# Splitting the last row block of three stage boundaries into halves of the tokens

## What is computed

```python
def rmsnorm(x, g):
    xf = x.astype(jnp.float32)
    y = xf * lax.rsqrt(jnp.mean(xf * xf, axis=-1, keepdims=True) + EPS)
    return y.astype(x.dtype) * g

def swiglu(x, w_gate, w_up, w_down):
    return (jax.nn.silu(x @ w_gate) * (x @ w_up)) @ w_down

# first block
h = h + 0.5 * rmsnorm(swiglu(rmsnorm(h, ffn1_pre_g), w1_gate, w1_up, w1_down), ffn1_post_g)   # then boundary 1
u = rmsnorm(h, mix_pre_g);  ... = split(u @ w_in)            # state-space branch, attention branch, gates
h = h + rmsnorm(merged @ w_out, mix_post_g)                                                   # then boundary 2
h = h + 0.5 * rmsnorm(swiglu(rmsnorm(h, ffn2_pre_g), ...), ffn2_post_g)                       # then boundary 3
# second block
u = rmsnorm_2(h, norm1_g);  proj = u @ w_in_2                # delta rule, sparse attention, gates, FFN
...
return rmsnorm_2(h, final_g)
```

## Time and profile before

| | us |
|---|---|
| time, median of 3 runs | 2542.17 (2541.75 to 2544.55) |
| profiled execution | 2541.03 |
| its span in the trace | 2539.2 |
| TensorE busy in the span | 2491.9 |
| VectorE, ScalarE busy | 1672.5, 1200.7 |
| mean granted TensorE clock | 0.997 of full |

### The profile page before, as it was taken

One profiled execution on the slowest core, in us unless ns is written; L12 is line 12 of the kernel. 1 busy time (PEld: TensorE's weight loads), 2 busy tenths in 40 slices (PEclk: granted clock), 3 DMA queues, 4 the chain that ended last, 5 costly groups with the idle time before them and its releaser, 6 DMA issues.

```text
span 2539.2 us, 37185 instructions
## 1 busy us (share of the span) xinstructions
PE 2491.9 (98%) x15074; PEld 2049.0 (81%) x15074; DVE 1672.5 (66%) x2651; ACT 1200.7 (47%) x1997; POOL 76.1 (3%) x114
## 2 busy tenths in 40 slices
PE   9999999999999999999999999999999999999998
PEld 7999878887877777877999878777776787888887
DVE  6888248856766656248887257766877666677733
ACT  6556235665536455346555246544333454444421
POOL 0111000000000000000110000000000000000000
PEclk9999999999999999999999999999999999999999
DMA  5776322222222212223775323211111221222232
GB/s 172 175 185 152 106 93 92 83 75 75 75 67 75 75 59 72 94 92 92 180 177 154 95 90 100 76 43 35 43 43 51 67 67 63 96 100 96 92 100 71
DMA packets 80523, 237.79 MB, mean 94 GB/s; under 512 B 8928, under 2 KB 10976, under 8 KB 80352
## 3 DMA queue, kind: packets, MB, share of 16 engines
q1 hardware_dynamic: 68832, 213.56, 26.1%
q0 software_dynamic: 10080, 18.35, 4.8%
q10 hardware_dynamic: 1440, 3.49, 0.4%
HBM read 233.27 MB, written 2.10 MB: 93 GB/s over the span
## 4 chain that ended last, share of the span: by engine, by line
PE 85%; DVE 9%; ACT 3%; issue 1%; DMA 1%; ACTq 0%; DVEq 0%; SPq 0%
PE bank L2084 20%; PE bank L2086 19%; PE bank L2085 19%; PE bank L2098 4%; PE bank L2100 4%; PE bank L2099 4%; PE bank L2328 2%; PE bank L2167 1%; DVE hl L2829 1%; DVE small L3184 1%; PE bank L2253 1%; ACT hl L2473 1%; ACT fB L2450 1%; DVE fB L3180 1%; PE bank L2234 1%
## 5 line engine op out<-in xcount | busy, mean ns | idle before, releaser
L2829 DVE TENSOR_TENSOR hl<-raw,hl 128x1024 fp32r<-128x1024 f32 (+2 forms) x325 | 386.0, 1191 | 471.5 <-ACT hl L2473 470.3
L2084 PE MATMUL bank<-uR,hl 128*128 128x512 f32 x1696 | 691.5, 408 | 2.8 <-DVE uR L2840 2.3
L2086 PE MATMUL bank<-uR,hl 128*128 128x512 f32 x1696 | 662.7, 391 | 0.0
L2085 PE MATMUL bank<-uR,hl 128*128 128x512 f32 x1696 | 662.1, 390 | 0.0
L2473 ACT CAST hl<-raw 128x1024 fp32r<-128x1024 f32 (+2 forms) x325 | 329.9, 1020 | 218.4 <-PE bank L2086 212.0
L2084 PEld LDWEIGHTS bank<-uR,hl 128*128 128x128 f32 x1696 | 319.1, 188 | 95.6 <-issue 25.2
L2086 PEld LDWEIGHTS bank<-uR,hl 128*128 128x128 f32 x1696 | 318.8, 188 | 68.8
L2085 PEld LDWEIGHTS bank<-uR,hl 128*128 128x128 f32 x1696 | 319.2, 188 | 68.0 <-issue 7.2
L2823 DVE TENSOR_TENSOR hl<-raw,hl 128x1024 fp32r<-128x1024 f32 (+1 forms) x142 | 150.7, 1075 | 31.5 <-ACT hl L2469 27.8
L2098 PE MATMUL bank<-sum,hl 128*128 128x256 f32 x560 | 159.0, 284 | 1.2 <-DVE fA L2975 1.1
L2099 PE MATMUL bank<-sum,hl 128*128 128x256 f32 x560 | 158.4, 283 | 0.0
(11 more groups left out here) (502 smaller groups left out, 4240.1 us busy)
## 6 DMA issues: line engine op xcount, KB each, us to landing
raw<-in_win SPq DMA_DIRECT2D x147, 512.0 KB, 3.5
raw<-in_w SPq DMA_DIRECT2D x44, 512.0 KB, 3.4
raw<-in_w1u SPq DMA_DIRECT2D x54, 256.0 KB, 3.1
raw<-in_w2u SPq DMA_DIRECT2D x51, 256.0 KB, 3.4
raw<-in_w1g SPq DMA_DIRECT2D x22, 512.0 KB, 4.6
raw<-in_w2g SPq DMA_DIRECT2D x22, 512.0 KB, 4.6
raw<-in_w1d SPq DMA_DIRECT2D x16, 512.0 KB, 3.6
raw<-in_wssd SPq DMA_DIRECT2D x16, 512.0 KB, 3.4
```

The lines of the kernel that those rows point to most:

```text
L2084: e.matmul(s.bank[:, :], h[:, 0, w], hi, start=s.first and q == 0, stop=False)
L2085: e.matmul(s.bank[:, :], h[:, 0, w], lo, start=False, stop=False)
L2086: i = e.matmul(s.bank[:, :], h[:, 1, w], hi, start=False, stop=s.last and q == n - 1)
L2829: e.tensor_tensor(h[:, 1, w], x[:, w], h[:, 0, w].bitcast(F), ALU.subtract).then_inc(*sig("dve_split.lo", s, i))
```

## The change

At the three boundaries the last row block is computed for tokens 0 to 255 (call it half 0) and then for tokens 256 to 511 (half 1), with matmuls of 256 columns. The norm, the residual, the new input `uR` and the three leading panels go by these halves too. `keep(3)` is gone, `sum_first` and `post_fold` are replaced, and `collect` takes pairs of pages that lie in one tensor, so that a VectorE instruction can take two blocks of one half at once. New in the plan, in this order:

```diff
+    def mm_half(p, half, js, xs, bank, cut=slice(None)): ...   # ends[js[p]] = s, 0
+    def post_steps(T, half, pairs, at=()):
+        for n in range(5):
+            if n < 4:
+                ks = (2 * n, 2 * n + 1)
+                T["h"][half][n] = s = step("post_h", ks=ks, ..., last=T["last"][half], qs=T["qs"] if half else None, cols=halves[half])
...
+            if n:
+                T["lo"][half][n - 1] = s = step("post_lo", ks=(2 * n - 2, 2 * n - 1), ..., hi=T["h"][half][n - 1])
...
+            if n in at:
+                open_split(*at[n])
+    def half_sum(T, half):
+        s = step("last_sq", b=T["b"][half], bt=list(T["b"][half].t), q=T["q"], cols=halves[half])
+    def half_root(T, half, ready):
+        s = step("end_sum", b=T["sum"][half], q=T["q"], ready=ready, r=T["r"], cols=halves[half])
+    def last_rows(ys, tail, gpost, half, gpre):
...
+        for p in range(len(js)):
+            if p == len(js) - 1:
+                mm_half(p, 0, js, xs, T["b"][0], slice(0, 4))
+                for n in range(2):
+                    s = step("end_first", b=T["sum"][n], c=acc, cols=halves[n])
+                acc.release(("pe_end.first", s))
+                a_end = mm_half(p, 0, js, xs, T["b"][0], slice(4, None))
+            else:
+                mm_half(p, 0, js, xs, T["b"][0])
+        T["q"], T["r"] = fp.take(), fp.take()
+        sq = half_sum(T, 0)
+        mm_half(0, 1, js, xs, T["b"][1], slice(0, 4))
+        T["rt"][0], _ = half_root(T, 0, sq)
+        b_end = mm_half(0, 1, js, xs, T["b"][1], slice(4, None))
+        for p in range(1, len(js)):
+            b_end = mm_half(p, 1, js, xs, T["b"][1])
...
+        post_steps(T, 0, 4, {0: (js[0] + NHL,), 1: (js[0] + NHL + 1,)} if len(js) > 1 else {})
+    def boundary(T, srcs, normed, drop=None, con=None):
+        sq = half_sum(T, 1)
+        T["rt"][1], done = half_root(T, 1, sq)
+        js = [panel(srcs[0], KB * 128, False)]
+        open_split(js[0] + 2)
...
+        post_steps(T, 1, 4)
```

The engines' parts. On TensorE `lead` keeps its first lines, the wait for the splits of all three panels, and then:

```diff
+            def block(i, half, k):
...
+                e.matmul(b[:, cols], h[:, 0, w], uR[:, 0, k, cols], start=k == 0, stop=False)
+                e.matmul(b[:, cols], h[:, 1, w], uR[:, 0, k, cols], start=False, stop=False)
+                go.wait_ge(*on("dve_norm.lo", lo, k))
+                return e.matmul(b[:, cols], h[:, 0, w], uR[:, 1, k, cols], start=False, stop=k == KB - 1)
+            for i, ks in ((0, range(0, 6)), (2, range(0, 6)), (0, range(6, 8)), (2, range(6, 8))):
+                for k in ks:
+                    for n in ((0, 1), (), (2,))[i]:
+                        block(n, 0, k)
             for k in range(KB):
+                for n in range(3):
+                    i = block(n, 1, k)
+                    if k == KB - 1:
+                        i.then_inc(*sig("pe_gemm.mm", s, n))
```

ScalarE's `post_h` waits for the residual and writes two high parts of 256 columns; in half 1 it also squares both blocks, 512 wide. VectorE's `post_h` and `post_lo`:

```diff
+        def post_h(s):
...
+            if k < KB - 2:
+                i = e.tensor_tensor(y2, y2, two_r, ALU.mult)                  # two blocks x 256 tokens
+            else:
+                e.tensor_tensor(s.ys[k][:, s.cols], s.ys[k][:, s.cols], s.r[:, s.cols], ALU.mult)
+                i = e.scalar_tensor_tensor(out=s.ys[k + 1][:, s.cols], in0=s.b[:, s.cols], ...)
+            e.scalar_tensor_tensor(out=hT[:, k:k + 2, s.cols], in0=y2, scalar=0.5 if s.half else 1.0,
+                                   in1=hT[:, k:k + 2, s.cols], op0=ALU.mult, op1=ALU.add)
+        def post_lo(s):
+            for k in s.ks:
+                go.wait_ge(*on("act_norm.hi", s.hi, k))
+                e.scalar_tensor_tensor(out=uR[:, 1, k, s.cols], in0=hT[:, k, s.cols], ...)
```

More of the change, by code:

```diff
@@ L479, in build, with wide_pages, take_two, both_of @@
     open_split(0, 2)
+    def wide_pages(x, n):
+        bs = [x[:, i, :] for i in range(n)]
+        home.update({id(b): (x, i) for i, b in enumerate(bs)})
+        return bs
+    def take_two():
+        spots = [home[id(b)] for b, _ in fp.left]
+        for n, (x, i) in enumerate(spots):
+            for m, (y, j) in enumerate(spots):
+                if x is y and i < j:
+                    a, b = fp.left[n][0], fp.left[m][0]
+                    return [fp.take_of([a]), fp.take_of([b])]
+        raise RuntimeError("no two pages of one tensor")
+    def both_of(pages, cols):
+        (x, i), (y, j) = (home[id(p.b)] for p in pages)
+        return x[:, i:j + 1:j - i, cols]
     def load(src, width, half=0):
@@ L618, in collect @@
         ys.append(y)
[L620 to L632, removed]
+    halves = [slice(0, 256), slice(256, 512)]
@@ L633, in boundary @@
+    def boundary(T, srcs, normed, drop=None, con=None):
+        ys, gpre, half = T["ys"], T["gpre"], T["half"]
+        sq = half_sum(T, 1)
+        T["rt"][1], done = half_root(T, 1, sq)
+        T["q"].release(done)
+        js = [panel(srcs[0], KB * 128, False)]
+        open_split(js[0] + 2)
         if con is not None:
             con()
[L635 to L645, removed]
+        qs = T["qs"] = [fp.take_of(low)] + [fp.take() for _ in range(KB - 1)]
+        post_steps(T, 1, 4)
+        for n in range(2):
+            T["b"][n].release(("dve_post.y", T["h"][n][3]))
@@ L646, in boundary @@
+        r = T["r"]
+        r.release(("dve_post.y", T["h"][1][3]))
+        sq_t = [("act_norm.sq", T["h"][1][k // 2], k) for k in range(KB)]
         js += [panel(src, KB * 128, False) for src in srcs[1:3]]
         for part in range(2):
-            s2 = step("sq_sum", s=s, qs=qs, part=part, before=s2 if part else None)
+            s2 = step("sq_sum", need=sq_t[7 if part else 5], qs=qs, part=part, before=s2 if part else None)
             for k in ((1, 3, 5), (7, 2, 6, 4))[part]:
@@ L2147, in sum_first @@
[L2147 to L2150, removed]
+            def block(i, half, k):
+                hi, lo = s.T["h"][half][k // 2], s.T["lo"][half][k // 2]
+                w, cols = slice(k * 128, (k + 1) * 128), (slice(0, 256), slice(256, 512))[half]
+                b, h = s.bs[i], hs[i]
+                go.wait_ge(*on("dve_split.lo", splits[s.js[i]]))
+                go.wait_ge(*on("act_norm.hi", hi, k))
+                e.matmul(b[:, cols], h[:, 0, w], uR[:, 0, k, cols], start=k == 0, stop=False)
+                e.matmul(b[:, cols], h[:, 1, w], uR[:, 0, k, cols], start=False, stop=False)
+                go.wait_ge(*on("dve_norm.lo", lo, k))
+                return e.matmul(b[:, cols], h[:, 0, w], uR[:, 1, k, cols], start=False, stop=k == KB - 1)
```

198 lines of the change are left out of this document (100 added, 98 removed).

## The result

The changed kernel takes 2575.95 us (median of 4 runs, 2574.24 to 2578.09) against 2542.53 for the kernel before in the same runs: ratio 1.0131, 95% interval 1.0115 to 1.0147. It is slower by 33 us; 2578 was predicted. The span is 2575.9, which is 36.7 above the span of before, so the difference between these two profiled executions is between 3 and 4 us larger than the one between the medians.

What follows compares the result with a forecast made beforehand. TensorE, busy 98% of the span, was taken to bound the kernel. Boundary losses of 12.06, 11.28 and 12.40 us gave +35.7 on 2541.03, so 2576.8, and 2578 for the median; range 2560 to 2590, chance 0.65.

Steps and rivals of the forecast that it cites:

- Narrow row block: Last row block in 256-column halves: 17.14 us at boundaries 1 and 3 (1.27 more), 7.08 at boundary 2 (0.64 more).
- the leads: Leading panels at each boundary as 144 narrow matmuls: 17.35 us, +0.50, +0.83 and +0.85 at boundaries 1, 2, 3.
- The chain of half 0: ScalarE and VectorE steps after half 0's products, boundaries 1 and 3: half 1's square by 17.0 us, first leading product 21.0.
- Wait: TensorE idle before the first leading product: 12.64 us against 5.70 at boundary 1, 12.17 against 5.71 at boundary 2.
- the slow sum: Half 1's late sum over partitions run at the low clock before the lead: 0.3 us extra a boundary.
- Clock: Clock falls in each boundary's wait and the lead starts slow: 2.4 us a boundary, 2.7 with the slow sum.
- the rival in which the clock stays up: Sum or half products in the boundary gap keep the clock full: sum 27.6 us, 2570; chance 0.15.
- Resumption: From the lead's end to the next panel at each boundary: 0.94 us instead of 0.29, +0.65.
- The faster rival: Half 1's square comes early, splits hidden: 36.5 us at boundaries 1 and 3, 26.5 at 2; total 2536; chance 0.03.
- The splits don't stand in series: Rival: leading splits at boundaries 1 and 3 slip under residual work, 11 us less, 2567; chance 0.10.

Runs made afterwards that it cites:

- the kernel with narrow products alone: Kernel before with each of the 72 leading 512-column matmuls at each boundary made as two of 256, same block order; 2543.46 us, ratio 1.0012.
- the fill: Changed kernel with unread products put back into its two waits at each boundary, nine behind the last row block, three behind the late sum; 2570.71 us, ratio 1.0115.
- the reordered kernel: Changed kernel with half 1's square and sum and the third leading split earlier, leading products waiting for their own panel only; 2558.31 us, ratio 1.0067.
- the woven kernel: Changed kernel with ScalarE's copies and VectorE's subtractions placed separately, half 1's square and root earlier, own-panel waits, half 0's products four blocks at a time; 2541.76 us, ratio 1.0004.
- the small splits: Changed kernel with the first two leading panels' splits at boundaries 1 and 3 handling only 8 of 1024 columns; 2569.62 us, ratio 1.0110.

## Why the prediction was right

The sum was made from the trace: 35.7 us. The profiled executions differ by 37.1, the three stretches by 36.9, the medians by 33.4; the forecast of 2578 for the median lies 2 us above the measured one. By its own terms, for the profiled execution (predicted, measured at boundaries 1, 2, 3):

- *Narrow row block*: 17.14 and 7.08; 17.11, 7.26, 17.11. The pace by rows was borne out: in the kernel with narrow products alone the leads grew by 0.41, 0.70 and 0.73, where the prediction has 0.50, 0.83 and 0.85, and the whole by 3 us by the ratios. By the 2.5 ns between matmuls of the Trainium skill (TensorE: Matmul & The Clock Gate, section Back-to-back issue gap) it would have been 0.5 us in all; the measurement doesn't agree (at least 0.8 by the interval, 1.8 for the three leads in the trace).
- *The chain of half 0*: half 1's square was to end 17.0 us after half 0's products. At boundary 1 it ended at 371.24, and half 0's products were through at 354.27: 16.97. The steps on the way (4.45, 6.36, 7.6, 12.1, 15.7) are met within 0.1. At boundary 3 it took 17.35, because the first subtraction starts 0.47 us after its copy's end instead of 0.10; what held it is not shown. This is why the time came out: one plan order for both engines puts the leading splits and half 1's square into one chain, and the experiments that cut it at the square (2.2 us a boundary in the traces, 2.5 expected), at the root and third split (4.0, expected 3.5) and at the first two splits (4 at boundaries 1 and 3, expected 5.6) each moved the lead. By the ratios they gave 4, 10 and 5 us.
- *Wait*: 12.94, 12.47 and 12.94 with the slow sum; 13.38, 12.76, 13.72. The slow sum cost 0.5 and not 0.3 (L2198 lasts 1.22 against 0.70), and the first product starts 0.24 after the last subtraction, which the sum had at nothing.
- *Clock*: I took 2.4 for each lead; 1.7, 2.7 and 2.4 were measured (19.01, 20.01, 19.71 less 17.35). The mechanism is shown by the fill, and the rival in which the clock stays up is out: the window above has 0.50. That 2.4, taken from the kernel's start, came so near is in part luck, since the low stretches differ from place to place; by the ratios the clock's share may be down to 4 us.
- *Resumption*: 0.94; 0.95 at all three.
- *The faster rival* (halves that overlap as they suggest, 2536): by the plan's order its condition, ScalarE reaching half 1's square in time, did not hold, as the prediction says. In the reordered kernel the square of boundary 1 ended 1.9 us behind half 1's products, 10.2 us after half 0's, so the condition was nearly made true, and the gain stayed away (2558). In the woven kernel the square started 8.5 us after half 0's products, and then the rival's 36.5 us for boundaries 1 and 3 came near (37.28 and 37.19). At boundary 2 it had 26.5 and 31.55 was measured: there VectorE's residual work feeds the lead more slowly than TensorE multiplies, and the clock falls. I had left both out.
- *The splits don't stand in series* (2567): refuted by the small splits in the trace, though a part of what I charged to the splits was the wait for high parts ahead of the copy.

## What to carry to other kernels

These are lessons from one kernel. Before work is cut in halves to overlap it, write down for each engine what stands in its list between the first half's result and the second half's first step. Here buffers held for the second half moved two splits from under the matmuls into that chain, and a single plan order for two engines made each wait for the other. A filler that nobody reads is work: its 2.7 us in a wait of 5.7 kept the clock and were worth 8 us over three places. Halving paid, by 1.2 to 1.5 us, at the two boundaries where the second half is 8 us long, and not where it is 3 us. That the length decides is argued from these three places; a woven boundary 2 with its waits filled was not run.

## What the runs showed of the hardware

The clock did not fall at the same distance from the last matmul each time, nor come back at the same distance from the first. In one execution of the changed kernel it fell 3.5 us (366.1, from the mean of 0.76 in the window above), 5.2 and 2.0 us after the last row product, and the leads began at the low level for 3.8, 6.1 and 5.4 us. In the kernel before without its unread products it fell 4.2, 4.9 and 4.3 us after the last row product, with the two instructions of the sum in between. So the cost of a wait at the low clock varies from place to place. This is the likeliest reason why the profiled execution and the median give different shares for it; it was not tested. With a clock of 1.00 a 256-wide matmul costs 0.120 us and not half of the 0.227 of a 512-wide one, whether it reads the activations or a stage's input, and a weight load recorded at 0.19 beside each one does not hold it to 0.19.
